# A list planner lets TensorE wait a fifth of a dense piece for a chain step, in place of beginning the piece

## The chip, the cores and the metric

The kernel runs on one core of a Trainium2 chip. Its time is the device time of one launch in microseconds (us), taken as the median of several runs; one further run is profiled. TensorE, VectorE, ScalarE and GpSimd are called PE, DVE, ACT and POOL in the rows, the queue that starts transfers is SP.

## The reference, cut to what matters

Three blocks of one layer each follow one another over 512 tokens of width 1024, all in float32.

```python
def reference(x, ...):
    x = first_block(x, ...)    # norm, projections, Mamba2 scan + gated delta rule, gated merge, SwiGLU
    x = second_block(x, ...)   # norm, RWKV7 time mixing + attention over keys picked by an index, merge
    return third_block(x, ...) # SwiGLU, norm, gated MLP over chunks + differential attention, merge, SwiGLU
```

Two kinds of work are in each block. **Dense** products take the 512 tokens through a weight matrix (`h @ w_in`, `y @ w_out`, the SwiGLU). **Chains** are scans and attention over heads: many small products, each of which needs the one before it:

```python
def gdn_scan(q, k, v, g, beta):        # per head, chunks of 64 tokens
    kk = einsum(k, k); amat = where(strict, kk * decay * beta, 0)
    t = triangular_solve(eye + amat, concatenate([v * beta, k * beta * exp(gc)]))
    v_new = u - w @ state
    o = (q * exp(gc)) @ state + (q @ k.T * decay) @ v_new
    state = state * exp(gc_last) + (k * exp(gc_last - gc)).T @ v_new
```

The second block also scores keys for its sparse attention (8 index heads, four blocks of 128 queries) and takes the largest scores; the third takes softmax, a gelu and a root.

## The kernel before, in words

Every dense product of 512 tokens is made of tiles of 128 output features. A tile has 8 slices of 128 inputs (or 4, 22, 2), and each slice is three matmuls, since a float32 operand is split into a high and a low part: lines 1072 (high x high), 1073 (high x low) and 1074 (low x high), each 128x512. The plan's unit is a **dense piece**, two slices, so six matmuls. Weights come in panels by DMA from SP, are rounded on ACT (L2573) and their remainder is made on POOL (L2975).

The whole program is one list of steps. `order()` writes it, and each engine runs its part of it in that order, with semaphore waits where a step needs another. For most of the SwiGLU and output stages the list is written out by hand. In four **mixing stages** it comes from `weave(chains, *fills)`, a list planner: first the Mamba2 scan with the convolutions (stage A), then the gated delta heads (stage B), the RWKV pairs with the index scores and sparse attention (stage C), and the differential attention with the gated MLP (stage D). `weave` gets the chains, whose steps have parts on the engines, and the fills, dense tiles in order with the steps that take their results out of the two accumulator banks.

`SEG` holds the cost of each step's parts (`p1.36` is a dense piece on PE, `s.6` is 0.6 us on ACT). The planner keeps a clock `now` for each engine. In each round it takes, for each engine, the earliest moment at which a known part could start (`offers`), and for PE also the earliest dense piece (`stream`). The earliest offer is put into the list; among parts that are ready then, the one with the longest tail of dependants goes first. The dense piece is taken on PE only if it could start before the first chain part:

```python
        if stream and stream[0] < offers.get("p", 1e9):
            offers["p"] = stream[0]
```

So before the change a dense piece is begun whenever PE would stand idle, however shortly, and the chain part that becomes ready behind it waits for the piece's end. A tile's first piece needs a free accumulator bank and what `room` lists; the later pieces of a tile need nothing in the plan.

Names used below: L1120 (`blocks64`), L1106 (`transpose4`) and L1112 (`quad`) are the small products of the chains: 16 of 64x64 or 4 of 128x128. L1226 and L1363 to L1376 are steps of the delta scan. L1408 is `ixs`, one index score, 128 queries of one head against 256, 384 or 512 keys, taken out by ACT (L2777) and added up by DVE (L2199); L2209 and L2211 on DVE are the search for the largest scores (`ixt`), which the plan runs only when DVE is idle. L1478 to L1515 are the RWKV scan. In stage D L1569 is a query-key product, L2886 the exponential on ACT, L1578 and L1587 the transposes of its result and their product with the values, L1602 (`gs`) the MLP's product over tokens, with L2446 and L2450 its two DVE instructions, L2931 a gelu on ACT, and L1621 (`ft1p`) the sum of squares that ends a head, fed by L2946 (ACT), L2517 (DVE) and L2951 (ACT); L2522 and L2524 (DVE), L2956 (a root on ACT), L2530 and L2532 follow it. L1746 is the low part of an operand split. An ACT_TABLE_LOAD stands on ACT wherever its next function is in another table than the last.

## Time and profile before

| | us |
|---|---|
| median of 3 runs | 3038.27 |
| lowest, highest | 3038.21, 3054.9 |
| the profiled execution | 3034.87 |
| its span, first to last instruction | 3033.1 |
| PE busy in the span | 2962.9 |
| DVE, ACT, POOL busy | 1583.6, 1077.8, 1408.2 |

The first matmul of a mixing stage's first dense piece starts at 25.5 us (A), 245.09 us (B), 1174.74 us (C) and 2203.5 us (D), and the last dense piece of the stage at 243.93, 695.34, 1753.68 and 2579.22 us. The four stages are thus some 1,630 us of the span; the rest is written out by hand. A matmul's busy time in the rows overlaps that of the next, so a dense matmul reads as 0.39 us although the next one starts 0.23 us after it; what PE spends is read from start to start, and a wait shows as idle time only where it is longer than that overlap.

### The profile page before, as it was taken

To read this page: it belongs to the slowest core of one execution; us is meant where nothing else is said; L and a number is where in the kernel's file an instruction comes from. 1 tells how busy PE (TensorE), PEld (TensorE's weight loads), DVE (VectorE), ACT (ScalarE), POOL (GpSimd) and SP (SyncE) were. 2 spreads that over 40 slices of the span, in tenths; PEclk is the share of its full clock that TensorE was granted. 3 is DMA by queue.
4 is the path that set the end of the run, shared out by engine and by line. 5 is a ranking of instruction groups with operands and counts; after the bars stand their busy time and mean duration, and the time that the engine had idled before them with its cause. 6 is when DMAs were issued, how large, how long until landed. Compare 5 with 4: busy or idle time off the path is not lost.

```text
span 3033.1 us, 42345 instructions
## 1 busy us (share of the span) xinstructions
PE 2962.9 (98%) x16912; PEld 2381.4 (79%) x16912; DVE 1583.6 (52%) x3162; ACT 1077.8 (36%) x1784; POOL 1408.2 (46%) x1805
## 2 busy tenths in 40 slices
PE   6999999999999999999999999999999999999999
PEld 5778887877888887767877778888877778888887
DVE  5776557565666316559744453333275773333310
ACT  4453334333222223323324432222354554332221
POOL 4554444335555554314333365555444334555553
PEclk9999999999999999999999999999999999999999
DMA  3211212112344422102112222223321112222232
GB/s 127 83 55 64 70 57 65 61 48 94 127 144 147 125 91 67 37 22 70 36 46 73 71 83 97 95 95 100 110 77 63 56 63 91 86 95 97 98 103 85
DMA packets 72069, 248.02 MB, mean 82 GB/s; under 512 B 8128, under 2 KB 8512, under 8 KB 71744
## 3 DMA queue, kind: packets, MB, share of 16 engines
q1 hardware_dynamic: 71872, 245.30, 25.0%
q8 instruction: 134, 2.20, 0.3%
q14 instruction: 63, 0.52, 0.1%
HBM read 243.18 MB, written 2.10 MB: 81 GB/s over the span
## 4 chain that ended last, share of the span: by engine, by line
PE 88%; DVE 9%; ACT 2%; issue 1%; POOL 0%; DMA 0%; SPq 0%; DVEq 0%; ACTq 0%
PE bank L1072 24%; PE bank L1074 24%; PE bank L1073 24%; PE bank L1106 3%; PE bank L1120 3%; PE bank L1569 1%; PE bank L1083 1%; PE bank L1587 1%; PE bank L1578 1%; DVE t L2211 1%; DVE sm L2209 1%; PE bank L1457 1%; PE bank L1112 0%; DVE t L1790 0%; PE bank L1490 0%
## 5 line engine op out<-in xcount | busy, mean ns | idle before, releaser
L2975 POOL TENSOR_TENSOR R<-W,R 128x256 fp32r<-128x256 f32 x1715 | 1301.4, 792 | 1510.0 <-ACT R L2573 1509.9
L1072 PE MATMUL bank<-u,R 128*128 128x512 f32 (+1 forms) x3440 | 1389.5, 404 | 13.3 <-DVE u L1746 3.2
L1074 PE MATMUL bank<-u,R 128*128 128x512 f32 (+1 forms) x3440 | 1347.4, 392 | 0.0
L1073 PE MATMUL bank<-u,R 128*128 128x512 f32 (+1 forms) x3440 | 1345.4, 391 | 0.0
L1072 PEld LDWEIGHTS bank<-u,R 128*128 128x128 f32 (+1 forms) x3440 | 648.1, 188 | 160.5 <-issue 11.0
L1074 PEld LDWEIGHTS bank<-u,R 128*128 128x128 f32 (+1 forms) x3440 | 646.9, 188 | 141.7 <-issue 0.8
L1073 PEld LDWEIGHTS bank<-u,R 128*128 128x128 f32 (+1 forms) x3440 | 648.8, 189 | 128.0 <-issue 5.0
L2573 ACT ACTIVATE R<-W 128x1024 fp32r<-128x1024 f32 (+2 forms) x452 | 451.3, 1005 | 140.1 <-PE bank L1074 132.7
L2603 ACT ACTIVATE u<-t 128x512 fp32r<-128x512 f32 x126 | 78.3, 630 | 305.7 <-DVE t L1768 249.6
L1779 DVE SCALAR_TENSOR_TENSOR X<-bank,X 128x512 f32<-128x512 f32 x32 | 22.1, 692 | 239.0 <-PE bank L1074 239.0
L1754 DVE TENSOR_TENSOR t<-bank,t 128x512 f32<-128x512 f32 x66 | 45.5, 689 | 174.4 <-PE bank L1074 164.5
L1746 DVE TENSOR_TENSOR u<-t,u 128x512 fp32r<-128x512 f32 x126 | 99.3, 799 | 55.3 <-ACT u L2603 54.9
L2610 ACT ACTIVATE t<-t 128x512 f32<-128x512 f32 x66 | 41.7, 633 | 239.2 <-DVE t L1754 239.2
L1106 PE MATMUL bank<-CN,t 128*128 128x128 f32 x816 | 121.3, 279 | 3.6 <-DVE t L2092 1.7
L1768 DVE TENSOR_TENSOR t<-t,bank 128x512 f32<-128x512 f32 x66 | 45.3, 687 | 130.2 <-PE bank L1074 128.8
L1106 PEld LDWEIGHTS bank<-CN,t 128*128 128x128 f32 x816 | 91.4, 141 | 25.7 <-DVE t L2092 2.9
L1120 PEld LDWEIGHTS bank<-t,t 64*64 64x64 f32 x2560 | 83.3, 134 | 31.5 <-issue 26.1
L1120 PE MATMUL bank<-t,t 64*64 64x64 f32 x2560 | 98.3, 222 | 0.7 <-ACT t L2692 0.6
L1790 DVE SCALAR_TENSOR_TENSOR t<-bank,sm,t 128x511 f32<-128x511 f32 (+2 forms) x108 | 80.7, 747 | 26.5 <-ACT t L2619 23.9
L2129 DVE SCALAR_TENSOR_TENSOR t<-t,bank 128x512 f32<-128x512 f32 x48 | 32.8, 684 | 93.9 <-PE bank L1074 93.8
L2597 ACT ACTIVATE u<-X,PC 128x512 fp32r<-128x512 f32 x32 | 23.1, 723 | 149.9 <-DVE X L1779 149.9
L2886 ACT ACTIVATE t<-t,sm 128x128 f32<-128x128 f32 (+3 forms) x96 | 61.9, 647 | 31.0 <-DVE sm L2366 30.6
(395 smaller groups left out, 2741.1 us busy)
## 6 DMA issues: line engine op xcount, KB each, us to landing
W<-in_in SPq DMA_DIRECT2D x48, 512.0 KB, 3.3
W<-in_ff_in SPq DMA_DIRECT2D x44, 512.0 KB, 3.3
W<-in_g_qkv SPq DMA_DIRECT2D x24, 512.0 KB, 3.3
W<-in_ada SPq DMA_DIRECT2D x24, 512.0 KB, 3.3
W<-in_f1g SPq DMA_DIRECT2D x22, 512.0 KB, 3.3
W<-in_f1u SPq DMA_DIRECT2D x22, 512.0 KB, 3.2
W<-in_f2g SPq DMA_DIRECT2D x22, 512.0 KB, 3.2
W<-in_f2u SPq DMA_DIRECT2D x22, 512.0 KB, 3.2
```

Of the source, the lines that this page charges most:

```text
L1072: e.matmul(b[0:cols, :], wh, hi, start=(k == 0), stop=False)
L1073: e.matmul(b[0:cols, :], wh, lo, start=False, stop=False)
L1074: i = e.matmul(b[0:cols, :], wl, hi, start=False, stop=(k == KT - 1))
L1106: i = e.transpose(b[:, m * 128:m * 128 + 128], x[:, m * 128:m * 128 + 128], C("ident"))
L1120: i = e.matmul(b[g, s], l[g, s], x[g, s], start=True, stop=True)
L1746: e.tensor_tensor(r(lo[k]), t(src[k]), r(hi[k]).bitcast(F32), SUB).then_inc(*PR.dve.up("lo", tag, k))
L1754: e.tensor_tensor(t(FS[j % 4]), bank[BANK[name, j0 + j]], t(RB), MUL).then_inc(*FF.dve.up("got", name, j0 + j))
L1790: e.scalar_tensor_tensor(out=c[:, s:512], in0=b[:, 0:512 - s], scalar=half(wname, (3 - s) * nt + gj), in1=c[:, s:512], op0=MUL, op1=ADD).t ...
L2573: e.activation(R[q % NH][:, 0:n], W[p % NW][:, 0:n], ACT.Copy).then_inc(*PN.act.up("hi", key))
L2603: e.activation(r(hi[k]), t(src[k]), ACT.Copy).then_inc(*PR.act.up("hi", tag, k))
L2886: e.activation(ex, ex, ACT.Exp, bias=c[:, 0:1], scale=small[q.nw][:, 32 + 2 * qb + m:33 + 2 * qb + m], accum_out=c[:, 1:2]).then_inc(*AT.a ...
L2975: i = e.tensor_tensor(R[q % NH][:, 1024 + a:1024 + b], W[p % NW][:, a:b], R[q % NH][:, a:b].bitcast(F32), SUB)
```

## The change: the dense piece gives way to a chain part that is about to be ready

A constant `PATIENCE` of 0.3 is added, and in the planner's test the dense piece's earliest start is taken 0.3 us later than it is. It is then begun only if no chain part becomes ready on PE within 0.3 us. If one does, PE is left waiting for it, and the dense piece follows. Only pieces of dense tiles have this; the index scores and the MLP products that also open a bank (`OPENERS`) are compared as before. When a piece is chosen, it still starts at `stream[0]`.

```diff
-IN_SIGHT, FIRST = 12, 40.0
+IN_SIGHT, FIRST, PATIENCE = 12, 40.0, 0.3
...
-        if stream and stream[0] < offers.get("p", 1e9):
+        if stream and stream[0] + (PATIENCE if stream[1][0] == "dense" else 0.0) < offers.get("p", 1e9):
             offers["p"] = stream[0]
```

No instruction computes anything else. All four lists are planned anew, on every engine. On PE, the 10,320 dense matmuls stand in 407 unbroken runs before and in 367 after. In the planner's own account of the four stages, the PE parts of chains that start after a gap of at most 0.3 us number 10 before and 146 after (10, 60, 63 and 13 in A to D).

The first place is on PE early in stage B, where the inversions for heads 0 and 1 begin. Before:

```order
L1112 MATMUL bank7<-t55_104,t50_99 128x128 x4
L1112 MATMUL bank6<-t49_98,t50_99 128x128 x4
L1120 MATMUL bank2<-t45_94,t44_93 64x64 x8
L1072 MATMUL bank0<-u37_158,R0 128x512
L1073 MATMUL bank0<-u67_188,R0 128x512
L1074 MATMUL bank0<-u37_158,R0 128x512
L1072 MATMUL bank0<-u38_159,R0 128x512
L1073 MATMUL bank0<-u68_189,R0 128x512
L1074 MATMUL bank0<-u38_159,R0 128x512
L1120 MATMUL bank3<-t51_100,t45_94 64x64 x8
L1106 MATMUL bank4<-CN,t45_94 128x128 x4
```

After (the pair of L1112 stands further up):

```order
L1106 MATMUL bank6<-CN,t55_104 128x128 x4
L1120 MATMUL bank2<-t45_94,t44_93 64x64 x8
L1072 MATMUL bank1<-u12_133,R3 128x512
L1073 MATMUL bank1<-u13_134,R3 128x512
L1074 MATMUL bank1<-u12_133,R3 128x512
L1072 MATMUL bank1<-u14_135,R3 128x512
L1073 MATMUL bank1<-u15_136,R3 128x512
L1074 MATMUL bank1<-u14_135,R3 128x512
L1120 MATMUL bank3<-t51_100,t45_94 64x64 x8
L1120 MATMUL bank5<-t57_106,t56_105 64x64 x8
L1106 MATMUL bank4<-CN,t45_94 128x128 x4
```

Head 1's steps (bank 5 and bank 6, t56 to t58) now stand directly among head 0's (banks 2 to 4), where dense pieces stood between them, and the dense pieces at this point are earlier ones of the fill.

The second place is on PE in stage C, where the index scores end. Before, 11 of the 24 are spread among the steps of the RWKV scan, and the last 13 stand unbroken:

```order
L1408 MATMUL bank<-t_75,t_72 128x384
L1408 MATMUL bank<-t_75,t_73 128x384 x2
L1408 MATMUL bank<-t_75,t_74 128x384 x2
L1408 MATMUL bank<-t_75,t_71 128x512 x2
L1408 MATMUL bank<-t_75,t_72 128x512 x2
L1408 MATMUL bank<-t_75,t_73 128x512 x2
L1408 MATMUL bank<-t_75,t_74 128x512 x2
```

After, the scan's steps stand closer together, 4 scores are among them, and 20 stand unbroken:

```order
L1408 MATMUL bank<-t_75,t_73 128x256 x2
L1408 MATMUL bank<-t_75,t_74 128x256 x2
L1408 MATMUL bank<-t_75,t_71 128x384 x2
L1408 MATMUL bank<-t_75,t_72 128x384 x2
L1408 MATMUL bank<-t_75,t_73 128x384 x2
L1408 MATMUL bank<-t_75,t_74 128x384 x2
L1408 MATMUL bank<-t_75,t_71 128x512 x2
L1408 MATMUL bank<-t_75,t_72 128x512 x2
L1408 MATMUL bank<-t_75,t_73 128x512 x2
L1408 MATMUL bank<-t_75,t_74 128x512 x2
```

Four scores of 256 keys and three of 384 have moved into the unbroken run.

The third place is on ACT in stage D, where the first two heads (0 and 1) of the attention end. Before:

```order
L2951 ACTIVATE t48_97<-t48_97 128x512
L2886 ACT_TABLE_LOAD
L2886 ACTIVATE t52_101,sm<-t52_101,sm 128x512
L2886 ACTIVATE t53_102,sm<-t53_102,sm 128x512
L2931 ACT_TABLE_LOAD
L2931 ACTIVATE t70_119<-bank1 128x512
L2956 ACT_TABLE_LOAD
L2956 ACTIVATE t43_92<-t43_92 128x512
L2895 ACTIVATE t54_103<-bank5 128x512
L2946 ACTIVATE t35_84<-bank7 128x512
L2603 ACTIVATE u12_133<-t69_118 128x512
L2603 ACTIVATE u13_134<-t70_119 128x512
```

After:

```order
L2931 ACT_TABLE_LOAD
L2931 ACTIVATE t69_118<-bank0 128x512
L2956 ACT_TABLE_LOAD
L2956 ACTIVATE t43_92<-t43_92 128x512
L2886 ACT_TABLE_LOAD
L2886 ACTIVATE t52_101,sm<-t52_101,sm 128x512
L2886 ACTIVATE t53_102,sm<-t53_102,sm 128x512
L2931 ACT_TABLE_LOAD
L2931 ACTIVATE t70_119<-bank1 128x512
L2895 ACTIVATE t54_103<-bank5 128x512
L2946 ACTIVATE t35_84<-bank7 128x512
L2603 ACTIVATE u12_133<-t69_118 128x512
```

Head 0's root (L2956) now stands ahead of head 1's last exponentials (L2886). Over the whole program ACT has 24 table loads where it had 19, all five new ones in stage D. On DVE at this place one of the two pairs L2446, L2450 has moved from ahead of L2517 to behind it.

## Rows read from the trace of the kernel before

**Rows 1.** The page: the span, and busy time by engine with its share.

```profile
span 3033.1 us, 42345 instructions
PE 2962.9 (98%) x16912; PEld 2381.4 (79%) x16912; DVE 1583.6 (52%) x3162; ACT 1077.8 (36%) x1784; POOL 1408.2 (46%) x1805
```

**Rows 2.** Windows: stretch, length, busy PE, PEld, DVE, ACT, POOL; clock, DMA, GB/s.

```profile
33.00:229.00 196.00, 185.98 (x992) 149.37 (x993) 140.11 (x225) 91.12 (x174) 102.78 (x120) 0.98 0.21 68
229.00:700.00 471.00, 463.48 (x3520) 377.02 (x3519) 304.72 (x607) 167.63 (x323) 193.30 (x237) 1.00 0.19 60
1160.00:1345.00 185.00, 184.14 (x1739) 141.56 (x1738) 106.88 (x235) 59.74 (x106) 64.88 (x76) 1.00 0.14 44
1345.00:1375.00 30.00, 25.78 (x75) 14.45 (x74) 24.88 (x51) 12.86 (x21) 7.96 (x10) 0.77 0.11 35
1375.00:1758.00 383.00, 377.04 (x2758) 295.05 (x2757) 234.42 (x607) 141.88 (x266) 146.29 (x189) 1.00 0.19 60
2203.00:2295.00 92.00, 87.74 (x459) 65.97 (x460) 70.03 (x178) 55.31 (x106) 40.71 (x48) 1.00 0.22 72
2295.00:2305.00 10.00, 6.94 (x25) 5.24 (x26) 8.09 (x10) 3.89 (x7) 2.80 (x4) 0.83 0.12 37
2305.00:2580.00 275.00, 271.41 (x1310) 207.88 (x1308) 165.05 (x468) 128.55 (x245) 111.24 (x144) 1.00 0.22 70
```

**Rows 3.** Waits of PE in stages B and D: us in total, times, longest.

```profile
PE bank L1106 <- DVE t L2092: 1.7, 3, 1.3
...
PE bank L1621 <- ACT t L2951: 3.9, 3, 3.1
PE bank L1578 <- DVE t L2388: 3.5, 7, 0.9
```

**Rows 4.** Timeline of PE in stage B: start, us, instruction, shapes, count.

```profile
660.19 0.40 PE L1073 MATMUL bank<-u,R 128*128 128x512 f32 x1
660.43 0.39 PE L1074 MATMUL bank<-u,R 128*128 128x512 f32 x1
660.75 0.68 PE L1120 MATMUL bank<-t,t 64*64 64x64 f32 x16
661.36 0.65 PE L1106 MATMUL bank<-CN,t 128*128 128x128 f32 x4
661.77 0.48 PE L1072 MATMUL bank<-u,R 128*128 128x512 f32 x1
662.09 0.39 PE L1073 MATMUL bank<-u,R 128*128 128x512 f32 x1
```

**Rows 5.** Timeline of PE in stage C, index scores among and behind the scan.

```profile
1316.44 0.70 PE L1408 MATMUL bank<-t,t 64*128 64x256 f32 x2
1317.07 0.44 PE L1490 MATMUL bank<-t,t 64*64 64x64 f32 x4
...
1326.10 0.91 PE L1408 MATMUL bank<-t,t 64*128 64x384 f32 x2
1326.94 0.43 PE L1478 MATMUL bank<-t,t 128*64 128x128 f32 x2
...
1355.99 11.08 PE L1408 MATMUL bank<-t,t 64*128 64x512 f32 x16 [2.92 <-ACT t L2777]
```

**Rows 6.** Timeline in stage D: DVE, then PE (in brackets idle before, releaser).

```profile
2294.74 0.68 DVE L2446 TENSOR_TENSOR t<-bank,t 128x512 f32<-128x512 f32 x1
...
2296.32 0.69 DVE L2446 TENSOR_TENSOR t<-bank,t 128x512 f32<-128x512 f32 x1
...
2299.05 1.13 PE L1621 MATMUL bank<-t,CN 128*128 128x512 f32 x2 [3.06 <-ACT t L2951]
```

**Rows 7.** Windows behind that wait, columns as in Rows 2.

```profile
2299.00:2302.00 3.00, 2.96 (x8) 2.06 (x9) 2.10 (x3) 0.94 (x1) 1.98 (x3) 0.73 0.00 0
2302.00:2305.00 3.00, 3.00 (x10) 2.38 (x10) 2.30 (x2) 0.68 (x2) 0.82 (x2) 0.70 0.41 123
```

**Rows 8.** Timeline of ACT in stage D.

```profile
2291.32 1.28 ACT L2956 ACT_TABLE_LOAD   x1
2292.62 0.63 ACT L2956 ACTIVATE t<-t 128x512 f32<-128x512 f32 x1
```

## The prediction

> **What bounds the kernel now.** I read the page first: PE is busy for 2962.9 of 3033.1 us [rows 1]. A change in the order of work that removes nothing can win only what PE idles, and what it loses to a low clock. So I took the windows of the four mixing stages next. Window length minus PE busy is 10.0 us in A, 7.5 in B, 0.9 + 4.2 + 6.0 in C, and 4.3 + 3.1 + 3.6 in D: 39.6 us in all [rows 2]. That is the ceiling of any gain by better filling, 1.3% of the span, of which much is the start of a stage, where the fill can't help. The waits view says for whom PE waits in B and D: a handful of steps, 0.3 to 3.1 us each [rows 3]. The timelines then give the price of a change of work on PE, of an index score, and of the two places where the new order differs most.
>
> The rest of the span, dense work in a fixed order, is not planned anew and costs nothing more or less.
>
> **Term 1, the added waits.** The planner's account has 136 more gaps of up to 0.3 us in front of chain parts. Bounds: 0, if the chain part is ready anyway when PE comes to it, and 136 x 0.3 = 40.8 us. If the gaps are spread evenly between 0 and 0.3, their mean is 0.15, together 20.4 us (an estimate). Against it stands that PE is slower than the planner's costs: in a run of dense matmuls the spacing is 0.24 (660.19 to 660.43), but from the last dense matmul to L1120 it is 0.32, and from the first dense one behind a chain step to the second 0.32 again (661.77 to 662.09) [rows 4]. Six matmuls at 0.23 are the planner's 1.36 us; a dense run costs up to 0.18 us more, which is not in its costs, while the chain's work on DVE and ACT goes on. So where a dense run stands between two steps of a chain, a planned wait of 0.15 us is eaten. Where only another chain's steps stand there, it is real. The first place of the change shows both. The nearest row of waits that the plan did not cover is L1578 for L2388, 3.5 us over 7 times [rows 3], so in D I expect more than the plan says. I take a third of the mean, 0.05 us each: **+6.8 us**, bounds 0 and 20.4 (40.8 at the very most).
>
> **Term 2, stalls that go.** With the chain further ahead, the three waits of L1106 in B (1.7 us) should mostly go. In D, PE waits 3.06 us for L2951 before L1621 at 2299.05 [rows 6]. In the new order one pair L2446, L2450 no longer stands ahead of L2517, which feeds L2951; two pairs follow each other by 1.58 us there (2294.74 to 2296.32), so the wait should shrink by about 1.6 us. What is late next there is the pair's L1746, which drops behind the reciprocal L2524; its reader comes much later in the list. Behind that wait the clock granted is 0.73 and 0.70 for 6 us [rows 7], that is, part of the time at 1.2 GHz instead of 2.4; at full speed 6 x 0.285 = 1.7 us less. I take half of it. Together 1.7 + 1.6 + 0.8: **-4.1 us**, bounds 0 and -6.5 (1.7 + 3.1 + 1.7).
>
> **Term 3, fewer changes of work.** There are 40 fewer dense runs. Each had up to 0.09 us extra on either side [rows 4], 7.2 us in all. But a change from one kind of chain step to the next isn't free either: L1106 behind L1120 takes 0.41 up to the dense matmul, L1120 takes 0.61 with 16 of 64x64 whatever follows. I take 0.05 us a run: **-2 us**, bounds 0 and -7.2.
>
> **Term 4, the index scores.** Among the scan's steps a score costs PE 0.63 us with 256 keys and 0.84 with 384. In the unbroken run at the end, 16 matmul records for 8 scores of 512 keys take 11.08 us, 1.38 each [rows 5], with PE at clock 0.77 over the stretch and DVE busy for 24.9 of 30 us [rows 2]: each score waits for its bank, and DVE fills up with the search. The change moves 4 scores of 256 and 3 of 384 from the cheap place to the dear one. By width (my estimate, 1.38 x 1/2 and x 3/4, rounded up for DVE's share of the search) they cost 0.72 and 1.18 there: 2.9 + 3.5 - 4 x 0.63 - 3 x 0.84 = **+1.4 us**. Bounds: 0, and all seven at 1.38, 9.7 - 5.0 = +4.7. DVE's scan steps that sit ahead of them stay as they were.
>
> **Term 5, table loads.** ACT gets five more, 1.28 us each, and the next ACTIVATE starts 1.30 after the load starts [rows 8]: 6.5 us more on ACT, which is busy 36% of the span. The cover is dense work on PE; it is gone where the load stands in a head's path, as ahead of head 1's last exponentials, where L1578 and then L1621 wait. I take **+1 us**, bounds 0 and 6.5. The Trainium skill, page "ScalarE: Activation LUTs", section "What ACT_TABLE_LOAD costs", gives 1283 ns for the load and adds a drain of about 1380 ns, 2.66 us a switch. The row has the same load but no drain behind it; by the page the upper bound would be 13.3 us instead of 6.5.
>
> **Costs nothing.** DMA issues, panel rounding and POOL's remainders move with the dense pieces, their number is the same. A dense run grows by a tenth (10,320 matmuls in 367 runs, not 407), and POOL is busy 52% of stage A and less of the others [rows 2], so panels are in time. If that cover went, it would be one wait of PE for a panel at a time.
>
> **Sum.** 6.8 - 4.1 - 2 + 1.4 + 1 = +3.1 us. The profiled execution took 3034.87 us (its span 3033.1 and 1.8 around it), so 3038.0 on that scale. The median of the runs is 3.4 us above the profiled one; on the median's scale it is 3038.3 + 3.1 = 3041.4 us, **0.1% slower**, which a measurement of this kernel can't tell from no change: about 1% is what it can tell, that is below 3008 or above 3069 us.
>
> **Rivals.**
>
> *The stalls go and the waits don't come* (chance 0.17). If nearly all added waits are eaten by the dense runs' unplanned cost, Term 1 is near 0, Term 3 goes to -7.2 and Term 2 to -6.5: 3038.3 - 13.7 + 1.4 = 3026 us. For it: in B, PE idled only 7.5 us in 471 although chains and fill are woven tightly. Against: the plan now aims at the very moment of readiness, with no slack.
>
> *The waits are real, and slower* (0.18). Where several chain steps stand in a row, as at the first place, no dense run hides anything. Then the mean of 0.15 us is paid 136 times, the scores and the table loads cost their upper bounds, and Term 2 yields half: 20.4 + 4.7 + 6.5 - 2 - 2 = +27.6, 3066 us at the top, 3055 at the middle of this case. It decides from about 0.1 us a wait. For it: in D the waits for L2388 were 0.5 us each, longer than planned ones. Against: that is 7 waits in a stage whose idle time comes to 11 us of 377 [rows 2].
>
> *The clock falls* (0.04), the rival that is slower by over 1%. Place: the stretches of C and D where waits stand close together. Price: 6 us at about 0.71 cost 1.7 us [rows 7]; added to the case above it takes two or more such falls to pass 3069, some 16 if it came alone. Against: in B, with 7.5 us of idle time in small pieces, the clock was 1.00 throughout [rows 2]; it fell only behind a wait of 3 us. The Trainium skill, page "TensorE: Matmul & The Clock Gate", section "A second HAM failure mode: psum-queue depth-cycling", speaks against this change: a PE that idles briefly between groups often enough is said to swing between its two clocks. By that rule the time would be this rival's; by B's row it isn't.
>
> *The planner's waits change nothing at all* is part of the forecast: the fill sets the stage's end, and its 10,320 matmuls are the same.
>
> **How the numbers follow.** Forecast 0.61 (3032 to 3050), rivals 0.17, 0.18 and 0.04. The range leaves out the far ends of both first rivals: 3029 to 3056 us. It holds all of the forecast, the nearer part of the gain case and the middle of the slower one; that one of the three runs took 3054.9 us for the same kernel is a reason not to end lower. Faster by over 1% would need 30 of the 39.6 us: 0.01. Slower by over 1%: the clock's 0.04. Within 1%: 0.95.
>
> **What would show it.** Waits of PE: many more of them in B and C, each under 0.3 us, the total of B up by 2 to 4 us; fewer than three for L2092; the wait of L1621 for L2951 near 1.5 us where it was 3.06. PE's idle time over the four stages 38 to 48 us. The unbroken L1408 stretch longer by 5 to 10 us, the scan before it shorter by about 5. Table loads 24. The clock in B still 1.00. I am wrong if the idle time grows by over 15 us, if PE waits for panels, or if the stage lengths move by over 5 us without idle time that explains it.

## The result: 20.8 us slower, and the profile after

The changed kernel takes 3059.18 us (median of 14 runs, 3056.69 to 3065.92) against 3038.38 of the kernel before on the same chip (14 runs): ratio 1.0062, 95% interval [1.0051, 1.0074]. The forecast was 3041.4, its range ended at 3056. The profiled execution took 3057.2 us where that of before took 3034.87: +22.3. The sign was right; of the forecast's +3.1 us nearly seven times as much came.

The page of the changed kernel, its span and busy times, answers to [rows 1]:

```profile
span 3055.4 us, 42355 instructions
PE 2966.4 (97%) x16912; PEld 2389.0 (78%) x16912; DVE 1599.7 (52%) x3162; ACT 1085.2 (36%) x1789; POOL 1399.2 (46%) x1805
```

The span grew by 22.3 us and PE's busy time by 3.5: PE mostly stands idle longer. ACT's five more instructions are the table loads. DVE executes the same 3162 instructions and is busy 16 us longer, which was in no term.

To place the loss I measured each stage from its first dense matmul to its last, and summed the idle times that the timeline shows inside it (PE, us; what a matmul's overlap hides isn't in them):

```
            A       B       C       D     between and around
before    218.4   450.3   578.9   375.7
after     228.4   453.6   584.7   377.8
change    +10.0    +3.3    +5.8    +2.1     +1.1
idle       10.0     4.7     7.7    10.3     before
idle       17.0     9.4    10.8    12.5     after
```

How far one execution can be trusted: in other profiled executions, where a stage had the plan of before, A took 217.1 to 222.6 us (six of them), B 450.2 or 450.3, C (without the clock effect told below) 580.4 to 582.1, D 375.6 to 376.7. So A's +10 is good to some 4 us, and C's +5.8 may be nearer to 4. In A the granted clock goes with the length: the two executions of 222.2 and 222.6 us had a mean clock of 0.96 there, as the changed kernel has, and that of 217.1 us had 0.99. Against an execution of the same clock, A is some 6 us longer.

Windows of the changed kernel, the four stages and the index scores; columns as in [rows 2], to which they answer:

```profile
25.70:255.10 229.40, 212.28 (x1110) 168.07 (x1111) 158.64 (x259) 102.35 (x192) 112.37 (x132) 0.96 0.19 63
255.20:709.40 454.20, 444.41 (x3419) 364.66 (x3417) 293.27 (x579) 161.57 (x313) 188.84 (x230) 1.00 0.18 59
1355.00:1385.00 30.00, 29.44 (x69) 15.80 (x70) 26.09 (x60) 13.55 (x23) 8.31 (x10) 0.62 0.11 36
1188.40:1773.80 585.40, 574.31 (x4487) 443.32 (x4486) 367.11 (x880) 205.80 (x382) 205.94 (x257) 0.98 0.16 51
2223.80:2602.20 378.40, 365.37 (x1792) 279.64 (x1792) 243.63 (x653) 194.55 (x359) 149.18 (x196) 1.00 0.21 69
```

B and D keep their clock of 1.00, A is at 0.96. In A the plan has the fewest waits: 10, of 2.1 us in all, against 60 of 8.8 us in B. A's price is not a count of waits.

Waits of PE in the changed kernel, in the order A (three rows), B (three), C (one), D (two); those of L2092, L2388 and L2951 answer to [rows 3]:

```profile
PE bank L1155 <- DVE t L1833: 5.8, 1, 5.8
PE bank L1083 <- ACT t L2682: 4.6, 3, 3.7
PE bank L1072 <- DVE t L1790: 2.4, 1, 2.4
...
PE bank L1072 <- DVE t L1790: 3.3, 3, 1.6
PE bank L1106 <- DVE t L2092: 2.0, 3, 0.9
PE bank L1120 <- DVE t L1941: 1.7, 4, 0.7
...
PE bank L1097 <- DVE sm L1668: 4.7, 4, 2.3
...
PE bank L1578 <- DVE t L2388: 8.9, 9, 2.5
...
PE bank L1621 <- ACT t L2951: 0.8, 1, 0.8
```

The plan meant to wait 0.27 us before L1155 and 0.22 us before the L1083 that waits 3.7; before L1072 it planned no wait. PE waits over ten times as long there. L2682 is the square that heads the norm of the Mamba2 output, L1790 the convolution, L1668 the last of the ten small DVE instructions of a **root** (lines 1646 to 1668, each 128 partitions by 4 to 16 numbers); C's L1097 reads one.

### The profile page after: what moved, and what is told of

Read it like the earlier page. It is cut to its first block, busy times and chain, and to the rows that moved or that the text cites. A ratio compares the mean times of both kernels' runs of the same rounds, so it can differ in the third digit from the quotient of the medians.

```text
span 3055.4 us, 42355 instructions
## 1 busy us (share of the span) xinstructions
PE 2966.4 (97%) x16912; PEld 2389.0 (78%) x16912; DVE 1599.7 (52%) x3162; ACT 1085.2 (36%) x1789; POOL 1399.2 (46%) x1805
## 4 chain that ended last, share of the span: by engine, by line
PE 85%; DVE 11%; ACT 2%; issue 1%; POOL 1%; DMA 0%; SPq 0%; DVEq 0%; ACTq 0%
PE bank L1072 24%; PE bank L1074 23%; PE bank L1073 23%; PE bank L1106 3%; PE bank L1120 3%; PE bank L1569 1%; PE bank L1083 1%; DVE t L1790 1%; PE bank L1587 1%; PE bank L1408 1%; PE bank L1578 1%; DVE sm L1661 0%; PE bank L1112 0%; PE bank L1457 0%; PE bank L1490 0%
## 5 line engine op out<-in xcount | busy, mean ns | idle before, releaser
L1072 PE MATMUL bank<-u,R 128*128 128x512 f32 (+1 forms) x3440 | 1387.9, 403 | 17.9 <-DVE t L1790 5.7
L1072 PEld LDWEIGHTS bank<-u,R 128*128 128x128 f32 (+1 forms) x3440 | 648.3, 188 | 167.6 <-issue 15.1
L1106 PE MATMUL bank<-CN,t 128*128 128x128 f32 x816 | 119.6, 278 | 4.9 <-DVE t L2092 2.0
L1106 PEld LDWEIGHTS bank<-CN,t 128*128 128x128 f32 x816 | 91.8, 141 | 24.7 <-DVE t L2092 3.7
L1790 DVE SCALAR_TENSOR_TENSOR t<-bank,sm,t 128x511 f32<-128x511 f32 (+2 forms) x108 | 80.7, 747 | 24.7 <-ACT t L2619 22.0
L2886 ACT ACTIVATE t<-t,sm 128x128 f32<-128x128 f32 (+3 forms) x96 | 62.0, 647 | 31.2 <-DVE sm L2366 30.9
```

The source lines that it names most:

```text
L1072: e.matmul(b[0:cols, :], wh, hi, start=(k == 0), stop=False)
L1106: i = e.transpose(b[:, m * 128:m * 128 + 128], x[:, m * 128:m * 128 + 128], C("ident"))
L1790: e.scalar_tensor_tensor(out=c[:, s:512], in0=b[:, 0:512 - s], scalar=half(wname, (3 - s) * nt + gj), in1=c[:, s:512], op0=MUL, op1=ADD).t ...
L2886: e.activation(ex, ex, ACT.Exp, bias=c[:, 0:1], scale=small[q.nw][:, 32 + 2 * qb + m:33 + 2 * qb + m], accum_out=c[:, 1:2]).then_inc(*AT.a ...
```

## Where the time goes in stage A

PE's timeline at the three long waits, first of the kernel before, then of the changed one (the third has no counterpart before):

```profile
52.93 0.43 PE L1155 MATMUL bank<-t,CN 128*128 128x96 f32 x2 [3.48 <-DVE t L1833]
...
211.03 0.73 PE L1102 MATMUL bank<-u,CR 128*128 128x512 f32 x2
211.60 0.39 PE L1072 MATMUL bank<-u,R 128*128 128x512 f32 x1
...
215.46 1.05 PE L1083 MATMUL bank<-CN,t 128*128 128x1 f32 x8 [2.34 <-ACT t L2682]
```

```profile
48.64 0.71 PE L1155 MATMUL bank<-t,CN 128*128 128x96 f32 x2 [5.80 <-DVE t L1833]
...
183.82 0.80 PE L1072 MATMUL bank<-u,R 128*128 128x512 f32 x1 [2.44 <-DVE t L1790]
184.42 0.63 PE L1073 MATMUL bank<-u,R 128*128 128x512 f32 x1
184.85 0.63 PE L1074 MATMUL bank<-u,R 128*128 128x512 f32 x1
...
217.19 0.73 PE L1102 MATMUL bank<-u,CR 128*128 128x512 f32 x2
221.62 1.87 PE L1083 MATMUL bank<-CN,t 128*128 128x1 f32 x8 [3.71 <-ACT t L2682]
```

Before, one dense piece (1.4 us, six matmuls from 211.60) stood between L1102 and L1083. The rule took it out of there, because the planner thought L1083 almost ready; the wait grew from 2.34 to 3.71 us, which is that very piece. A wait for L1833 was there too and grew from 3.48 to 5.80, with four dense pieces in front of it where seven stood. Why the planner took L1833 for almost ready can be read from its price: `SEG` has `sums="p.32 v2.0 s.69"`, so 2.0 us on VectorE, and in the kernel before the ten instructions from L1822 to L1833 take 4.3 us, with a GpSimd remainder beside the later ones:

```profile
48.58 0.21 DVE L1822 TENSOR_SCALAR t<-t 128x96 f32<-128x96 f32 x1 [1.46 <-ACT t L2646]
...
52.70 0.19 DVE L1833 COPY t<-t 128x64 f32<-128x64 f32 x1
```

The second cost is the clock behind such a wait: dense matmuls start 0.43 us apart (184.42 to 184.85) where full speed is 0.23, and L1083 takes 1.87 instead of 1.05. The windows around the three places, of before and then of the changed kernel (columns as above; the clock is the third figure from the end):

```profile
46.00:56.00 10.00, 6.52 (x28) 4.84 (x27) 7.18 (x17) 3.58 (x7) 3.65 (x6) 0.92 0.36 122
176.00:196.00 20.00, 19.32 (x104) 14.15 (x102) 16.41 (x27) 9.51 (x20) 12.74 (x14) 1.00 0.24 80
216.00:236.00 20.00, 19.34 (x134) 15.66 (x134) 8.63 (x11) 8.96 (x18) 13.05 (x16) 1.00 0.18 56
```

```profile
46.00:56.00 10.00, 7.36 (x24) 6.09 (x25) 5.75 (x13) 1.58 (x2) 1.50 (x3) 0.66 0.28 103
176.00:196.00 20.00, 17.50 (x95) 13.40 (x94) 13.78 (x27) 6.37 (x11) 9.12 (x12) 0.91 0.18 59
216.00:236.00 20.00, 15.64 (x101) 12.48 (x98) 11.60 (x15) 7.19 (x16) 6.76 (x8) 0.83 0.08 27
```

Counted over stage A, 37 dense matmuls start 0.38 us or more behind the dense one before them, where before had 23: 3.4 us more of lost time. With 7.0 us more idle that is this pair's 10 us. Of the two only the idle time is the change's for certain. With the plan of before in A, the kernel with the rule in D alone has 36 such matmuls, that with the rule in B alone 19; one plan loses more clock in one execution than in another. The Trainium skill, page "TensorE: Matmul & The Clock Gate", section "A second HAM failure mode: psum-queue depth-cycling", blames frequent small idle gaps in the kernel that it describes. These rows don't show that: B has the most and the smallest gaps and kept 1.00; the clock fell in A at three waits of 2.4 to 5.8 us.

Why the planner was wrong on L1790 shows on DVE. Rows of before, then of the changed kernel, the same two instructions of a root, with GpSimd's piece of the changed kernel last:

```profile
171.05 0.17 DVE L1650 TENSOR_SCALAR sm<-sm 128x8 int32<-128x8 int32 x1
171.46 0.17 DVE L1654 TENSOR_TENSOR sm<-sm 128x8 f32<-128x8 f32 x1
```

```profile
175.05 0.66 DVE L1650 TENSOR_SCALAR sm<-sm 128x8 int32<-128x8 int32 x1
176.44 0.67 DVE L1654 TENSOR_TENSOR sm<-sm 128x8 f32<-128x8 f32 x1
...
174.94 2.84 POOL L2975 TENSOR_TENSOR R<-W,R 128x256 fp32r<-128x256 f32 x4 [0.84 <-ACT R L2573]
```

The chain of ten took 1.9 us before (170.65 to 172.52) and 4.8 us after (174.65 to 179.47), because GpSimd made remainders beside it. The planner has one price for it. Over the whole program the roots have 450 instructions. With GpSimd idle one takes 0.17 us. In the kernel before 110 of them overlap a GpSimd instruction and take 0.62 us on average, in the changed one 167, at 0.56; so all the roots took 127.2 us and now take 143.5. A plan that begins a dense piece in every gap has up to 1.4 us of slack in front of most chain steps without meaning to, and this absorbed such errors. A plan that aims at the moment of readiness has none.

## Experiments: which stage

**One stage at a time.** Each kernel uses the new rule in one stage; the others have their plan of before. The edit, here for A:

```diff
-def weave(chains, *fills):
+def weave(chains, *fills, patience=0.0):
...
-        if stream and stream[0] + (PATIENCE if stream[1][0] == "dense" else 0.0) < offers.get("p", 1e9):
+        if stream and stream[0] + (patience if stream[1][0] == "dense" else 0.0) < offers.get("p", 1e9):
```

with `patience=PATIENCE` in the one call of `weave` and 0.0 in the others.

> The waiting rule holds in stage A alone (Mamba2 scan and convolutions); B, C and D are planned as before. Local theory (each stage's loss is its own, from the waits that its own plan adds): stage A was 10.0 us longer with the change, so about +10 us over the kernel before. Rival theory, the forecast's own account (136 added waits, each worth about the same): A has 10 of the 146, so about +1 us. Rival theory, spread over the whole program (a changed interleaving disturbs whatever follows): less than +5 us here, and the four single-stage kernels do not add up to +21.

> The waiting rule holds in stage B alone (gated delta heads), which has 60 of the 146 planned waits. Local theory: +3.4 us, the stage's own lengthening. Equal price per wait: 60/146 of 21, about +9 us. If the stages add up, the four kernels give about +21 together.

> The waiting rule holds in stage C alone (RWKV pairs, index scores, sparse attention), 63 of the 146 waits. Local theory: +5.8 us, of which the longer unbroken run of index scores is 1.4 and waits for the 4x4 root's tiny DVE instructions (L1668) about 4. Equal price per wait: +9 us.

> The waiting rule holds in stage D alone (differential attention and gated MLP), 13 of the 146 waits, and it has the five added table loads. Local theory: +2.1 us: about +5 from PE waiting for L2388, -3 from the wait of L1621 for L2951 that has shrunk. Equal price per wait: +2 us, so this run does not tell those two apart; it tells whether a gain in D is there (below 0) or not.

Medians: A 3056.28, ratio 1.0031 [1.0009, 1.0053]; B 3042.59, 0.9998 [0.9978, 1.0019]; C 3042.80, 0.9993 [0.9978, 1.0009]; D 3042.19, 0.9998 [0.9979, 1.0017] (12 runs each, before 35). These ratios can't be read alone: the runs of before on this chip fall into two groups, 19 from 3035.8 to 3040.8 and 16 from 3050.4 to 3055.1. Means of the lower groups: before 3038.6, A +8.9, B +3.8, C +4.0, D +2.8. The sum is +19.5, and the change has +20.4 by the same measure: **the stages' prices add up, and nearly half is A's**. An equal price per planned wait, as the forecast had it, would have given A about +1 and B and C about +9 each. C alone had no run in an upper group; A had 6 of 12, B 2, D 3.

**Stage A, dense pieces given back before one or three kinds of step.** The rule in A, except where the chain step waited for is `sums` (which reads what L1833 makes), and then also `sn1p` and `sn2p` (the norm with L1083 and the root):

```diff
+        chained = min(jobs["p"], key=lambda x: x[0])[1][0] if jobs["p"] else None
-        if stream and stream[0] + (patience if stream[1][0] == "dense" else 0.0) < offers.get("p", 1e9):
+        if stream and stream[0] + (patience if stream[1][0] == "dense" and chained not in ('sums', 'sn1p', 'sn2p') else 0.0) < offers.get("p", 1e9):
```

> Stage A's waiting rule, but not where the next chain part is a step of the opening softplus chain (sums). Compared with the kernel before, undisturbed by the clock in stage C, stage A alone cost 10.6 us in its profile. Theory (a dense piece taken from in front of a wait that the plan prices too low makes that wait longer and lets the clock fall behind it): the wait of L1155 returns from 5.8 to about 3.5 us and the low clock behind it goes, so stage A is about 3 us shorter than with the full rule in A: +7 to +8. Rival (the loss in A comes from the other engines' new order, not from PE's waits): no change, still +10.

> As the last, and also not before the sums of squares that end a group of heads (sn1p, sn2p). Theory: the wait of L1083 for L2682 returns from 3.7 to about 2.3 us and the low clock behind it goes, 3 to 4 us more: stage A at +3 to +5. Rival (other engines' order): still near +10. With nothing left of the rule there would be 0.

Medians 3046.85, 1.0028 [1.0008, 1.0048], and 3042.87, 1.0018 [0.9998, 1.0037]; means of the lower groups +8 and +4, both as expected. Stage A goes 229.0 (rule throughout), 226.6, 223.2, 218.4 (before; 217.1 to 222.6 in other executions). The waits went back to 3.5 us (L1155) and 2.3 (L1083), as expected. The clock didn't follow the first of them: its mean over A is 0.96 with the rule and 0.96 without `sums`, and 0.98 only in the second kernel. Of the 10 planned waits 7 are given back, and with them more than half of A's loss; the wait for L1790 stays at 2.4.

**A third of the patience.** 0.1 us in A, B and D, none in C: `patience=0.1` in three calls.

> The dense piece waits for a chain step up to 0.1 us instead of 0.3 in stages A, B and D, and not at all in C. The plan then has 4, 19 and 3 waits of 0.2, 1.4 and 0.2 us in all (10, 57 and 13 of 2.1, 8.8 and 2.5 in the change). If the price lies in where the plan leaves a chain step no room, and not in the number of waits, stage A's length falls most of the way back: 218 to 221 us where the change has 228, B 451 to 453 and D 375.5 to 377. If any use of the rule in A costs the same, A stays at 225 or more.

One execution: A 220.0, as expected, B 452.3, as expected, D 379.7, which neither case had: one wait of L1578 for L2388 came to 5.5 us, with only 3 waits planned in the stage, none before L1578. ACT's rows tell of it: ahead of that head's last exponentials stood a root (L2956), a table load, a gelu, and the exponentials' own load (2297.56 to 2301.42). The changed kernel has the same at its third place, with a wait of 1.95 us behind two loads:

```profile
2309.83 1.28 ACT L2956 ACT_TABLE_LOAD   x1
...
2311.78 1.28 ACT L2886 ACT_TABLE_LOAD   x1
2313.07 0.82 ACT L2886 ACTIVATE t<-t,sm 128x512 f32<-128x512 f32 x1
...
2316.59 0.66 PE L1578 MATMUL bank<-CN,t 128*128 128x128 f32 x4 [1.95 <-DVE t L2388]
```

So D shows the same thing as A, steps priced too low: `SEG` has no price for a table load, and `sb="v1.0"` for what takes DVE 1.65 us with 512 keys (L2382 to L2388, 2314.88 to 2316.53).

## Experiments: GpSimd beside VectorE

**Almost without GpSimd.** Kernel before, then the changed one, with all but 8 columns of each remainder piece left out from panel 16 on, so that the results are not the reference's:

```diff
             for a in range(0, n, 256):
-                b = min(a + 256, n)
+                b = min(a + 256, n) if q < 16 else a + 8
```

> The kernel before, but POOL makes only 8 of every 256 columns of the weight panels' low parts from the 17th panel on; those columns of the low parts are left out, so the result is not the reference's. POOL is then nearly idle. In the trace tiny DVE instructions (128x8) take 0.16 us beside an idle POOL and often 0.66 beside a busy one. Theory: they fall to 0.16 to 0.2 throughout, the 450 root instructions from 127 to about 95 us, and the kernel is 3 to 10 us faster because a few waits of PE are behind roots. Rival (the slow ones have another cause, such as the small table itself): their durations stay, the time too.

> The changed plan, with GpSimd making the remainder of only 8 columns in each piece of a panel from panel 16 on (the other columns are left out, so the results are not the reference's); the kernel before with the same cut took 3017.4. If small VectorE instructions drawn out beside busy GpSimd are a good part of why planned waits grow, the two plans come closer together: 3017.4 + 12 = about 3029 (between 3025 and 3033), the waits of L1097 for L1668 in stage C under 1.5 us (4.7 in the change), and the stall at L1072 in stage A near 184 us gone. If the change costs what it costs whatever GpSimd does, 3017.4 + 20.7 = 3038, with those waits as they are.

Before with the cut: 3017.37, ratio 0.9933 [0.9910, 0.9956], twice the gain that was expected at most. The roots' instructions fell from 127.2 to 81.5 us, idle PE in B from 4.7 to 1.5. So GpSimd's work beside DVE costs the kernel before up to 21 us. It isn't the small instructions' delay alone: DVE as a whole is busy 1431.7 us instead of 1583.6, and its instructions of over 16 columns have 93 us of the difference. The changed plan with the cut: 3029.17 (ten runs, 3026.8 to 3033.3), the waits of L1097 gone, C at 577.2, and the wait for L1790 in A down from 2.4 to 0.9 us. (That for L1833, among the first panels, which are whole, stays at 5.8.) The two plans are 11.8 us apart instead of 20.8 (on two chips whose runs of before have medians 0.6 apart), or 12.7 instead of 20.4 by the means of the lower groups. **Some 8 to 9 of the 20.8 us are GpSimd's delay on DVE's steps, no longer covered**; the rest stays without it. PE's waits that end with DVE say the same: 34.3 us before and 54.0 with the change, 26.0 and 36.3 with the cut. What of it small and what of it large instructions cost, no run separates. In D it wasn't GpSimd: the waits of L1578 for L2388 stay at 8.2 us.

**Length of GpSimd's pieces.** The loop's 256 as 128 and as 512, in the plan of before:

```diff
-            for a in range(0, n, 256):
-                b = min(a + 256, n)
+            for a in range(0, n, 128):
+                b = min(a + 128, n)
```

> The kernel before, with GpSimd's remainders (L2975) in pieces of 128 columns where it has 256: twice the instructions for the same elements. If a small VectorE instruction waits for the end of GpSimd's running instruction, the mean of the small ones beside busy GpSimd falls from 0.39 us to about 0.27, the root's instructions (L1646 to L1668) from 127 to about 105 us in all, and the time by half of what the near absence of GpSimd brought: -6 to -12, 3026 to 3032. If the delay has to do with the elements that GpSimd moves, or its fixed cost per instruction is what VectorE meets, 127 us or more and the time within 3 us of before, or 5 to 10 us above it where panels come late (GpSimd busy over 1,700 us).

> The kernel before, with GpSimd's remainders in pieces of 512 columns where it has 256. If a small VectorE instruction waits for the end of GpSimd's running instruction, it is drawn out further: mean beside busy GpSimd near 0.6 us, the root's instructions 160 us or more in all, and the time 8 to 20 us above before. If not, it stays at 127 us and within 3 us of before.

With 128: 3030.62, 0.9982 [0.9960, 1.0003]; seven runs from 3025.6 to 3031.2, five from 3044.5 to 3047.6. With 512: 3073.85, 1.0099 [1.0070, 1.0128]; of its four runs one is at 3059.4 and three near 3074. Group against group that is -10 and +21 or +22. One instruction of the root on DVE, all its 47 executions (min/median/max ns), in the kernel before, with the cut, with 128 and with 512:

```profile
L1648 DVE TENSOR_SCALAR sm<-sm x47: 169/176/717, 17.4 to 2676.3; 128x4 int32<-128x4 int32 x18, 128x8 int32<-128x8 int32 x17, 128x16 int32<-128x16 int32 x12
```

```profile
L1648 DVE TENSOR_SCALAR sm<-sm x47: 170/173/646, 18.8 to 2674.7; 128x4 int32<-128x4 int32 x18, 128x8 int32<-128x8 int32 x17, 128x16 int32<-128x16 int32 x12
```

```profile
L1648 DVE TENSOR_SCALAR sm<-sm x47: 170/177/439, 17.2 to 2666.6; 128x4 int32<-128x4 int32 x18, 128x8 int32<-128x8 int32 x17, 128x16 int32<-128x16 int32 x12
```

```profile
L1648 DVE TENSOR_SCALAR sm<-sm x47: 170/176/1270, 18.2 to 2715.3; 128x4 int32<-128x4 int32 x18, 128x8 int32<-128x8 int32 x17, 128x16 int32<-128x16 int32 x12
```

And GpSimd's piece with 128 and with 512 (count, busy us, mean ns):

```profile
L2975 POOL TENSOR_TENSOR R<-W,R 128x128 fp32r<-128x128 f32 x3428 | 1574.8, 496 | 1247.2 <-ACT R L2573 1247.0
```

```profile
L2975 POOL TENSOR_TENSOR R<-W,R 128x512 fp32r<-128x512 f32 x845 | 1123.3, 1351 | 1692.1 <-ACT R L2573 1692.0
```

The same 0.17 us of work takes at most 0.44, 0.72 and 1.27 us beside pieces of 496, 792 and 1351 ns: the longest delay is about one piece. The Trainium skill has a rule that fits, page "SBUF — State Buffer", section "Who interferes with whom": a DVE instruction with two inputs in SBUF, or one in a two-port mode, contends with a GpSimd instruction that reads SBUF, and whichever comes later in the two-port case blocks until the other ends. By these rows the length of the delay is as it says. L1648 has one input, and no row tells its mode; L1654, with two, takes at most 0.74 us before, 0.46 with 128 and 1.30 with 512.

The expectations were right on how long the delayed ones take and wrong on the sum. DVE's instructions of up to 16 columns that overlap a GpSimd instruction take 0.42 us on average before, 0.31 with 128 (expected 0.27) and 0.59 with 512 (expected 0.6). But all roots take 121.4 us with 128, not 105, and 126.2 with 512, not 160. Each piece holds up about one instruction, so longer pieces hold up fewer: 209 of the 450 root instructions overlap GpSimd with 128, 110 with 256, 58 with 512, at 0.38, 0.62 and 1.00 us. The root's total is therefore no reason for the time. DVE's total moves, through its wider instructions: 1530.7 us busy with 128 and 1640.5 with 512, against 1583.6, and PE's waits that end with DVE are 27.3 and 46.0 us against 34.3. Whether the longest single delays or the wider instructions make the time, no run tells apart.

## Experiments: stages C and D, and two groups of runs

**A dense matmul forced into the scan.** The plan of before, but in C the planner brings a dense piece forward once 10 us have gone by without one. The heart of the edit:

```diff
+        force = tired and bool(stream) and stream[1][0] == "dense" and stream[0] - lately[0] > densely and stream[0] <= offers.get("p", 1e9) + 0.01
```

> The kernel before, without any waiting rule. Only in stage C the planner prefers a dense piece once PE has gone 10 us of its own account without one, until 150 us into the stage; PE's stretch without a dense matmul in the RWKV scan (23 us in the trace of before) is split in two. The runs of before fall in two groups, about 3036 to 3041 and 3050 to 3055 us; in the profile of the stage-A kernel the clock was at 1.2 GHz for 35 us in just that stretch. Theory (the clock may or may not fall in that stretch, and stage C's new plan has none so long): all runs near 3038, no second group, mean 5 to 7 us below that of before, median 0 to 2 below. Rival (the second group has a cause outside stage C, or outside the order of work): two groups as before, a third to a half of the runs near 3052.

3041.67, 1.0006 [0.9990, 1.0023], twelve runs spread evenly from 3038.1 to 3051.5. The group was not removed but blurred: the 22.9 us without a dense matmul became 14.1 and 16.5 us, and in the profiled run the clock fell in the second of them. That second stretch holds 92 matmuls and is 16.5 us long only because of the low clock.

**The rule in C, but not before the root's reader**, `r2p` (the edit as above with `('r2p',)`):

> The rule in stage C alone (stages A, B and D planned as before), and there not where the waiting chain part is the one that reads the root (the step of L1097, spread2). Its plan has no planned wait on a root, so the 4.7 us of L1097 for L1668 should go: 3042.4 - 3 to 4 = 3038 to 3039.5 in the lower group. It also happens to put 11 scores among the scan's steps again and to have the stretch of 100 matmuls without a dense one that the kernel before has (57 where the rule holds throughout the stage). If that stretch is what gives the second group of runs, 14 to 16 us above, the group comes back: of 10 or more runs, 3 or more above 3050. If something else in the stage's old plan gave it, all runs lie below 3046, as with the rule in all of stage C.

3041.82, 1.0000 [0.9985, 1.0014], twelve runs from 3038.0 to 3044.1. The expectation was mistaken on the plan: this kernel's scan has no 22.9 us stretch, its longest is 12.9 as with the rule throughout. So it doesn't test that stretch by putting it back, but it is one more kernel without it. On the root it was half right: L1097's waits fell from 4.7 to 1.9 us, C from 585.2 to 584.0, the time by about 1. The unbroken run of scores is in this kernel too and is the likeliest part of what stays of C's price; no run takes it away alone. PE's timeline of the changed kernel there, which answers to [rows 5]:

```profile
1349.89 0.70 PE L1408 MATMUL bank<-t,t 64*128 64x256 f32 x2
1351.53 0.70 PE L1408 MATMUL bank<-t,t 64*128 64x256 f32 x4 [0.94 <-DVE t L2219]
1352.70 1.19 PE L1408 MATMUL bank<-t,t 64*128 64x256 f32 x4 [0.47 <-ACT t L2777]
1355.56 19.26 PE L1408 MATMUL bank<-t,t 64*128 64x384 f32 x30 [1.68 <-ACT t L2777]
```

24.9 us where before had 18.4, and behind it 7 dense matmuls at the lower clock where before had 3, 0.8 us more (0.62 in the windows above against 0.77 in [rows 2]).

**The upper group.** In all kernels whose scan has the stretch of 22.9 us without a dense matmul, runs fall into two groups whose means are 14 to 19 us apart: 6, 2, 3, 3, 3, 5 and 3 runs in the upper one of 12, 12, 12, 12, 12, 12 and 4 (A, B, D, the two of A with pieces given back, 128, 512), 1 of 6 with GpSimd's cut, and of before itself 16 of 35, 10 of 31, 7 of 29 and 4 of 17 on four chips. In the five kernels that have the rule in C (12.9 us) it is none of 12, 12, 10 and 12, and one of 14 in the changed kernel that stands apart at 3065.9, 7 above the median. Windows of that stretch, first in the profiled execution of before (lower group), then in that of the rule in A alone (upper group, 3067.1 us), both with the same plan there:

```profile
1308.00:1332.00 24.00, 24.00 (x207) 17.41 (x206) 13.23 (x43) 8.22 (x21) 0.00 (x0) 1.00 0.00 1
```

```profile
1320.00:1345.00 25.00, 25.00 (x140) 18.54 (x140) 8.82 (x30) 5.21 (x15) 0.00 (x0) 0.61 0.01 1
1345.00:1360.00 15.00, 15.00 (x73) 9.96 (x73) 4.38 (x13) 4.13 (x9) 1.23 (x2) 0.50 0.00 0
```

PE shows no idle time in either, and has half the clock in one of them: the stretch takes 37.1 us for 22.9, which is the 14 us between the groups. The two other profiled executions of an upper group (512, and before with GpSimd's cut) have 36.8 and 37.2 us there, the eight of a lower group 22.9 or 23.0. Why it falls in some executions isn't settled; the kernel's DMA and GpSimd are silent there in both. The length of the stretch alone doesn't settle it either: the clock fell in the forced kernel's stretch of 92 matmuls, and in none of the profiled kernels in the stretch of 12.9 us, which has 116.

**Stage D without its transposes.** The rule in D alone, not before `sc` (L1578).

> The rule in stage D alone, and there not where the waiting chain part is sc (L1578, the transposes that wait for VectorE's L2388). If the waits of L1578, 8.5 to 8.9 us with the rule and 3.5 without, are what stage D loses, they go back to 4 or less, the wait of L1621 for L2951 stays near 0.5 to 1, and stage D takes 373.5 to 375 us, less than before's 375.7. If ScalarE's added table loads cost it, it stays at 377 or more.

One execution: D 374.1 us, below the 375.7 of before, in the expected range, with 3 table loads more than before (ACT x1787 on the page; 5 more with the rule throughout). Waits of PE in D (lines stand one further down in this kernel):

```profile
PE bank L1579 <- DVE t L2389: 6.2, 5, 2.5
...
PE bank L1622 <- ACT t L2952: 0.3, 1, 0.3
```

The wait for L2951 is 0.3, so D keeps that gain. The transposes' waits fell from 8.5 only to 6.2, not to 4. The loads are not cleared: two of the five went too, and of the 6.2 us two waits, 1.96 and 0.96 us, still stand right behind a root and the exponentials' load on ACT. The longest, 2.5 us, has no load behind it: there L2388 is held up on DVE, by a pair L2446, L2450 that the plan put ahead of it.

**The two together.** The rule in C alone and GpSimd's pieces of 128.

> The rule in stage C alone, and GpSimd's remainders in pieces of 128 columns. The two effects were measured apart: the smaller pieces put the lower group of before at about 3028 (with five of twelve runs near 3045), and the rule in C gave +4 and no run in an upper group. If they add, all runs lie between 3028 and 3034, the median at 3031 to 3032, 0.2% below before's lower group; with the low clock of the upper group gone it is the most even of the versions. If the upper group has nothing to do with the stretch of the RWKV scan that holds no dense matmul (12.9 us with the rule, 22.9 without), some runs lie near 3046 again.

3032.97, ratio 0.9970 [0.9956, 0.9985], all twelve runs between 3030.5 and 3035.6, where the 17 of before on that chip lie from 3034.3 to 3053.6. Median and highest run are a little above the expected 3032 and 3034. It beats both kernels: 0.2% below before's lower group and 0.6% below its upper. Against the short pieces alone it gives 4 us away in the lower group (3028.3 to 3032.6 on two chips) and loses the upper one; the mean of all runs is 3032.8 against 3035.5.

## Why the prediction was wrong, point by point

**Term 1 is the step that failed.** It priced a wait by how long the planner meant it to be, at 0.05 us each and 20.4 us at most in reason. In A ten waits of 2.1 us in the plan cost 9 to 10 us, 7.0 of it idle time; in B 60 of 8.8 us cost 3.3. In place of the +6.8 us of the term, the four stages have 17.0 us more idle time. What a chain step costs is by how much its price in the plan is too low, as soon as the dense piece in front of it is gone: 3.71 for 2.34, 5.80 for 3.48, 2.44 for nothing. The prediction had the row that tells this, L1578 for L2388 "longer than planned", and dismissed it as seven small waits. It noted that the plan has "no slack", and costed that at nothing. The 17.0 us are past the 15 that it had named as the point at which it would be wrong. In A and D the underpriced steps are seen in the rows; what makes up B's 3.3 us was not isolated.

**Term 2, the stalls that go.** In B L1106 for L2092 stayed, 1.7 to 2.0 us. In D L2951's wait went further than forecast, 3.1 to 0.8 at the longest, so the reading of DVE's order was right. Its clock loss is gone from the dense matmuls behind it, and a stretch at half clock stands behind L1578's wait instead; those waits took the gain back, 3.5 to 8.9.

**Term 3, fewer dense runs.** Not seen: B has 21 fewer of them in the plan and got longer. No run isolates it.

**Term 4, the index scores.** Right: 13 scores in 18.4 us became 20 in 24.9, less 5.0 where they stood before, +1.5 (forecast +1.4). The clock behind it came on top, 0.8 us, which the term didn't have.

**Term 5, table loads.** 24, as read from the order. The place that the term named is where PE waits: 1.95 us before L1578 behind head 1's last exponentials, and 0.95 us behind a later root and load. The +1 was if anything too small, though stage D as a whole got shorter than before with three of the five.

**Costs nothing.** Wrong for GpSimd. Its remainders moved with the dense pieces, and the prediction asked only whether the panels would be in time. They were; but more pieces fell beside DVE's roots, and GpSimd's delay of DVE carries some 8 to 9 us.

**The rivals.** "The waits are real" had the right sign and spanned the measured time with its 3055 to 3066, by luck: it priced 136 waits alike, and took C's scores and D's loads at upper bounds that were never reached. "The clock falls" placed the falls in C and D; the largest came in A, 3.4 us in this pair, and executions of before's plan in A lost as much. B at 1.00 was right.

## What to carry to other kernels

When a static plan is tightened, don't count the gaps it adds; list the steps that the plan prices too low (compare each step's price with its longest duration in the trace, table loads included), and ask which filler stood in front of them. Filler before an underpriced step is slack that costs nothing, and taking it away costs the error, and at times the clock behind it. And where VectorE instructions on a critical chain run beside GpSimd, try shorter GpSimd instructions: the same elements in pieces half as long gave some 10 us between the lower groups of runs.

## What the runs showed of the hardware

- A VectorE instruction of 128x4 to 128x16 (L1648) takes 0.17 us, and beside a GpSimd subtraction up to about the length of one of its instructions: 0.44, 0.72 and 1.27 us with pieces of 128, 256 and 512 columns. Shorter pieces hold up more instructions for less time each, and the roots' total stays between 121 and 127 us.
- TensorE dropped to 0.50 of its clock with no idle time in the rows, in a stretch of 22.9 us that held only small float32 products, in some executions of the same plan and not in others; it cost 14 us. With the dense-free stretch at 12.9 us the times of four kernels (46 runs) show no such group; a stretch of fewer matmuls had the fall all the same, so the cause is open.
- The clock behind one and the same wait of PE can go either way: with the same plan in A the one before L1083 was 2.34 us with the clock at 1.00 in one execution (the window 216 to 236 above) and 2.33 us in the kernel with the rule in D alone, where this window holds the wait and what comes behind it:

```profile
214.00:234.00 20.00, 17.02 (x88) 13.50 (x87) 9.84 (x13) 7.05 (x15) 9.01 (x10) 0.83 0.08 27
```
